# Hybrid decoder block on one core: FFN gate and up products with the weights as the loaded operand

## The reference

```python
def rmsnorm(x, g):
    y = xf * lax.rsqrt(jnp.mean(xf * xf, axis=-1, keepdims=True) + EPS)
    return (y * g)
def swiglu(h, wg, wu, wd):
    return (jax.nn.silu(h @ wg) * (h @ wu)) @ wd      # wg, wu 2048 x 5632, wd 5632 x 2048
...
        x = x + 0.5 * swiglu(rmsnorm(x, ffn1_norm[i]), ffn1_wg[i], ffn1_wu[i], ffn1_wd[i])
        x = x + hybrid_mixer(rmsnorm(x, mix_norm[i]), ...)
        x = x + 0.5 * swiglu(rmsnorm(x, ffn2_norm[i]), ffn2_wg[i], ffn2_wu[i], ffn2_wd[i])
    return rmsnorm(x, final_norm)
```

## Time and profile before

| | |
|---|---|
| median of 3 runs | 1923.17 us (1922.71 to 1926.27) |
| span of the profiled execution | 1920.8 us |
| TensorE busy | 1906.4 us, 99%, 8715 matmuls |
| TensorE loads | 1562.8 us, 81% |
| VectorE busy | 997.9 us, 52% |
| ScalarE busy | 899.3 us, 47% |
| first FFN | to about 739 us |
| mixer | about 739 to 1188 us |
| second FFN | from about 1188 us |
| memory | 350.96 MB, mean 183 GB/s |

### The profile page before, as it was taken

The page is one execution under the profiler, slowest core; times in us unless marked ns, Lnnn a source line. Parts: engine busy times, 40 slices in busy tenths (PEclk is TensorE's granted clock), DMA queues, the critical chain, the costliest instruction groups (busy, mean ns, idle before and its releaser), DMA issues.

```text
span 1920.8 us, 23438 instructions
## 1 busy us (share of the span) xinstructions
PE 1906.4 (99%) x8715; PEld 1562.8 (81%) x8715; DVE 997.9 (52%) x1070; ACT 899.3 (47%) x1127; POOL 15.5 (1%) x24
## 2 busy tenths in 40 slices
PE   9999999999999999999999999999999999999998
PEld 7888888888888888887778778888888888888886
DVE  5445544544544444556665776544544445445444
ACT  6444444544444444444454546445444444444443
POOL 1000000000000000000000000000000000000000
PEclk9999999999999999999999999999999999999999
DMA  7555665566555556554435645665565555566664
GB/s 257 192 189 183 188 197 183 179 199 191 190 183 197 196 189 193 172 171 129 114 95 169 187 158 166 199 195 175 187 202 191 192 189 176 196 219 195 192 192 144
DMA packets 185947, 350.96 MB, mean 183 GB/s; under 512 B 13140, under 2 KB 17984, under 8 KB 185760
## 3 DMA queue, kind: packets, MB, share of 16 engines
q1 hardware_dynamic: 183264, 349.22, 56.8%
q10 hardware_dynamic: 2240, 0.47, 0.1%
q0 software_dynamic: 384, 0.47, 0.1%
HBM read 348.01 MB, written 2.10 MB: 182 GB/s over the span
## 4 chain that ended last, share of the span: by engine, by line
PE 97%; DVE 2%; ACT 1%; issue 0%; ACTq 0%; DVEq 0%
PE ps L459 30%; PE ps L461 30%; PE ps L460 30%; PE ps L480 3%; PE ps L625 1%; PE ps L645 1%; DVE w_lo L1164 1%; PE ps L626 0%; ACT w_hi L841 0%; PE ps L519 0%; PE ps L718 0%; DVE p_h L1433 0%; ACT junk L868 0%; DVE x L1229 0%; ACT hT_hi L855 0%
## 5 line engine op out<-in xcount | busy, mean ns | idle before, releaser
L1164 DVE TENSOR_TENSOR w_lo<-raw,w_hi 128x1024 fp32r<-128x1024 f32 x656 | 789.7, 1223 | 662.0 <-ACT w_hi L841 659.7
L841 ACT ACTIVATE w_hi<-raw 128x1024 fp32r<-128x1024 f32 x656 | 682.0, 1060 | 593.3 <-PE ps L461 517.2
L459 PE MATMUL ps<-w_hi,hT_hi 128*128 128x512 f32 x1760 | 690.9, 393 | 1.2 <-DVE w_lo L1164 1.1
L461 PE MATMUL ps<-w_hi,hT_lo 128*128 128x512 f32 x1760 | 685.6, 390 | 0.0
L460 PE MATMUL ps<-w_lo,hT_hi 128*128 128x512 f32 x1760 | 685.3, 389 | 0.0
L459 PEld LDWEIGHTS ps<-w_hi,hT_hi 128*128 128x128 f32 x1760 | 330.8, 188 | 69.1 <-issue 1.4
L461 PEld LDWEIGHTS ps<-w_hi,hT_lo 128*128 128x128 f32 x1760 | 330.4, 188 | 69.1
L460 PEld LDWEIGHTS ps<-w_lo,hT_hi 128*128 128x128 f32 x1760 | 330.7, 188 | 66.5
L459 PE MATMUL ps<-w_hi,guT_hi 128*128 128x512 f32 x704 | 274.5, 390 | 0.0
L461 PE MATMUL ps<-w_hi,guT_lo 128*128 128x512 f32 x704 | 274.0, 389 | 0.0
L460 PE MATMUL ps<-w_lo,guT_hi 128*128 128x512 f32 x704 | 273.9, 389 | 0.0
(11 more groups left out here) (197 smaller groups left out, 799.7 us busy)
## 6 DMA issues: line engine op xcount, KB each, us to landing
raw<-in_ffn_wg_dram SPq DMA_DIRECT2D x176, 512.0 KB, 4.5
raw<-in_ffn_wu_dram SPq DMA_DIRECT2D x176, 512.0 KB, 4.5
raw<-in_ffn_wd_dram SPq DMA_DIRECT2D x176, 512.0 KB, 4.7
raw<-in_w_in_dram SPq DMA_DIRECT2D x88, 512.0 KB, 3.8
raw<-in_w_out_dram SPq DMA_DIRECT2D x32, 512.0 KB, 4.5
raw<-in_cmp_k_w_dram SPq DMA_DIRECT2D x8, 256.0 KB, 3.3
raw<-in_cmp_v_w_dram SPq DMA_DIRECT2D x8, 256.0 KB, 4.0
out_dram<-y_fin SPq DMA_DIRECT2D x8, 256.0 KB, 3.1
```

The lines of the kernel that those rows point to most:

```text
L459: mm(o, x_hi, w_hi[:, s, kk, :], start=first and kk == 0, stop=False)
L461: ins = mm(o, x_lo, w_hi[:, s, kk, :], start=False, stop=last and kk == GK - 1)
L841: act.activation(w_hi[:, c % SLOTS, :, :], raw[:, c % SLOTS, :, :], ACT.Copy).then_inc(hi_ready, 1)
L1164: tt(w_lo[:, s, :, :], raw[:, s, :, :], w_hi[:, s, :, :].bitcast(F32), ALU.subtract).then_inc(lo_ready, 1)
```

## The change

For gate and up, the operands change places: the loaded operand is a 128x128 tile of the weights (w_hi or w_lo), the moving operand the 256 tokens of hT. The result has hidden features on the partitions and tokens along the bank, four tiles of 128 features in two banks, just as the down product wants it. `gu_transposes` and its banks' use go away. A group of these jobs is now 24 loads and matmuls of 256 columns, where it was 12 of 512.

The token scale rs now lies along the free axis. After the first gate job of each FFN a row form of it is made: VectorE spreads rs to rs_rows, TensorE transposes the two pieces into bank 7, ScalarE copies bank 7 to rs_cols. VectorE multiplies the gate result with rs_cols into gu (`gate`), ScalarE takes silu of gu in SBUF in one instruction, VectorE multiplies with the up result (`up`), ScalarE copies to guT_hi and VectorE makes guT_lo, all as 128x1024. The up result's own factor rs and the 0.5 are applied in the residual (half_rs, per token), since they are common to all hidden features of a token.

```diff
+        rs_rows_ready = sem("rs_rows_ready")
...
+            def ff_job(c, pair, i=None, per=0, after={}, before={}):
+
+                for j in range(JD):
+                    for f in before.get(j, ()):
+                        f()
+                    pe.wait_ge(lo_ready, count(c + j + 1, i, per))
+                    s = (c + j) % SLOTS
+                    for kk in range(GK):
+                        k = GK * j + kk
+                        for n in range(CH // P):
+                            o = ps[:, 2 * pair + n // 2, n % 2 * TOK:n % 2 * TOK + TOK]
+                            f_hi = w_hi[:, s, kk, n * P:n * P + P]
+                            f_lo = w_lo[:, s, kk, n * P:n * P + P]
+                            mm(o, f_hi, hT_hi[:, k, :], start=k == 0 and n % 2 == 0, stop=False, skip_group_check=True)
+                            mm(o, f_lo, hT_hi[:, k, :], start=False, stop=False, skip_group_check=True)
+                            ins = mm(o, f_hi, hT_lo[:, k, :], start=False, stop=k == KD - 1, skip_group_check=True)
+                    ins.then_inc(group_done, 1)
+                    for f in after.get(j, ()):
+                        f()
...
-            def gu_transposes(f, n, i=None):
-                pe.wait_ge(gu_done, count(2 * (NFC * f + n + 1), i, 2))
-                for b in range(2):
-                    to_bank(4 + b, operand_use("gu", f, b, n), i, 1)
-                    transposes(4 + b, [(kk * TOK + t * P, gu[:, t, (2 * b + kk) * P:][:, 0:P])
-                                       for kk in range(2) for t in range(NT)])
...
+            def rs_columns(f):
+
+                pe.wait_ge(rs_rows_ready, f + 1)
+                if f == 1:
+                    to_bank(7, seen[7])
+                for t in range(NT):
+                    ins = pe.transpose(ps[:, 7, t * P:t * P + P], rs_rows[:, t, :], ident)
+                ins.then_inc(rs_cols_full, 1)
...
-                job(c, JD, hT_hi, hT_lo, 0, after=after, before=before)
+                ff_job(c, 0, after=after, before=before)
+                rs_columns(f)
                 c += JD
                 with pe.Fori(0, NFC - 1) as i:
-                    job(c, JD, hT_hi, hT_lo, 1, i, 2 * JD)
-
-                    pe.wait_ge(silu_done, count(2 * (NFC * f + 1), i, 2))
-                    job(c + JD, JD, hT_hi, hT_lo, 0, i, 2 * JD, after={3: [lambda: gu_transposes(f, 0, i)]})
+                    ff_job(c, 1, i, 2 * JD)
+
+                    pe.wait_ge(gate_read, count(NFC * f + 1, i, 1))
+                    ff_job(c + JD, 0, i, 2 * JD)
+
+                    pe.wait_ge(gu_done, count(NFC * f + 1, i, 1))
...
+            def rs_columns(f):
+
+                act.wait_ge(rs_cols_full, f + 1)
+                act.activation(rs_cols[:, :], ps[:, 7, 0:TOK], ACT.Copy).then_inc(rs_cols_ready, 1)
+
+            def silu(f, n, i=None):
+
+                act.wait_ge(gate_read, count(NFC * f + n + 1, i, 1))
+                act.activation(gu[:, :, :], gu[:, :, :], ACT.Silu).then_inc(silu_done, 1)
...
                 job(c, JD, after=after)
+                rs_columns(f)
                 c += JD
                 with act.Fori(0, NFC - 1) as i:
-                    job(c, JD, i, 2 * JD, after={1: [lambda: silu(f, 0, c, i)]})
-                    job(c + JD, JD, i, 2 * JD, after={5: [lambda: gu_operand(f, 0, i)]})
+                    job(c, JD, i, 2 * JD, after={2: [lambda: silu(f, 0, i)]})
+                    job(c + JD, JD, i, 2 * JD, after={3: [lambda: gu_operand(f, 0, i)]})
...
+            def ffn_scales(f):
+
+                phase = RS_FFN2 if f else RS_FFN1
+                nc.vector.tensor_scalar(half_rs[:, f, :], rs[:, phase, :], 0.5, None, ALU.mult)
+                for t in range(NT):
+                    ins = nc.vector.tensor_copy(rs_rows[:, t, :], rs[:, phase, t:t + 1].to_broadcast([P, P]))
+                ins.then_inc(rs_rows_ready, 1)
+
+            def gate(f, n, done, i=None):
+
+                dve.wait_ge(group_done, count(done, i, 2 * JD))
+                dve.wait_ge(rs_cols_ready, f + 1)
+                tt(gu[:, :, :], ps[:, 0:2, :].rearrange("p b (k t) -> p (b k) t", t=TOK),
+                   rs_cols[:, :].unsqueeze(1).to_broadcast([P, CH // P, TOK]), ALU.mult).then_inc(gate_read, 1)
...
                 job(c, JD, after=after)
+                ffn_scales(f)
                 c += JD
                 with dve.Fori(0, NFC - 1) as i:
-                    job(c, JD, i, 2 * JD)
+                    job(c, JD, i, 2 * JD, after={1: [lambda: gate(f, 0, c, i)]})
                     job(c + JD, JD, i, 2 * JD, after={1: [lambda: up(f, 0, c + JD, i)],
-                                                      5: [lambda: gu_operand(f, 0, i)]})
+                                                      3: [lambda: gu_operand(f, 0, i)]})
...
-            half = lambda t: 0.5
+            halves = [lambda t: half_rs[:, 0, t:t + 1], lambda t: half_rs[:, 1, t:t + 1]]
```

More of the change, by code:

```diff
@@ L176, in build_program @@
     rs = sb("rs", [P, 6, NT])
+    half_rs = sb("half_rs", [P, 2, NT])
+    rs_rows = sb("rs_rows", [P, NT, P])
+    rs_cols = sb("rs_cols", [P, TOK])
     junk = sb("junk", [P, CONV], BF16)
@@ L288, in build_program @@
         rs_done = sem("rs_done")
+        rs_rows_ready = sem("rs_rows_ready")
+        rs_cols_full = sem("rs_cols_full")
+        rs_cols_ready = sem("rs_cols_ready")
+        gate_read = sem("gate_read")
         silu_done = sem("silu_done")
         gu_done = sem("gu_done")
+        gu_hi = sem("gu_hi")
+        gu_lo = sem("gu_lo")
         resid_done = sem("resid_done")
@@ L551, in ffn @@
                     else:
-                        before = {}
+                        if n == 1:
+                            pe.wait_ge(gu_done, NFC * (f + 1))
                         if f == 0:
@@ L878, in root @@
                 act.activation(var[:, phase, :], var[:, phase, :], ACT.Sqrt).then_inc(root_done, 1)
[L880 to L896 removed]
+            def rs_columns(f):
[4 more added lines that the diff above has]
+                act.activation(gu[:, :, :], gu[:, :, :], ACT.Silu).then_inc(silu_done, 1)
+            def gu_operand(f, n, i=None):
+                act.wait_ge(gu_done, count(NFC * f + n + 1, i, 1))
+                k = 4 * n
+                dst = guT_hi[:, k:k + 4, :] if i is None else guT_hi[:, bass.ds(i * 4 + k, 4), :]
+                act.activation(dst, gu[:, :, :], ACT.Copy).then_inc(gu_hi, 1)
             def ffn(f):
@@ L925, in ffn @@
                     if n == 0:
[L926 removed]
+                        after = {3: [lambda: gu_operand(f, NFC - 1)]}
                         if f == 0:
@@ L1264, in ffn @@
                     if n == 0:
-                        after = {1: [lambda: up(f, NFC - 1, c)], 5: [lambda: gu_operand(f, NFC - 1)]}
+                        after = {1: [lambda: up(f, NFC - 1, c)], 3: [lambda: gu_operand(f, NFC - 1)]}
                     else:
-                        after = {1: [lambda: residual(n - 1, c + JF * n, (n - 1) % 2, half)]}
+                        after = {1: [lambda: residual(n - 1, c + JF * n, (n - 1) % 2, halves[f])]}
                         if f == 0:
@@ L1549, in put @@
                     after.setdefault(c, []).extend(fs)
-                put(MIX0 + 1, lambda: residual(NDC - 1, MIX0, 1, half))
+                put(MIX0 + 1, lambda: residual(NDC - 1, MIX0, 1, halves[0]))
                 put(MIX0 + 3, lambda: variance(RS_MIX, DM, 2 * NDC))
@@ L1625, in _ @@
                 xs = x[:, t, DM - CH:DM]
-                stt(out=xs, in0=ps[:, 2 + t, :], scalar=0.5, in1=xs, op0=ALU.mult,
+                stt(out=xs, in0=ps[:, 2 + t, :], scalar=half_rs[:, 1, t:t + 1], in1=xs, op0=ALU.mult,
                     op1=ALU.add).then_inc(resid_done, 1)
```

70 lines of the change are left out of this document (24 added, 46 removed).

## The result

| | before | after |
|---|---|---|
| median, lowest to highest | 1922.94 us, 1922.71 to 1926.27 | 1972.71 us, 1972.24 to 1972.88 |
| span of the profiled execution | 1920.8 us | 1970.4 us |
| matmuls on TensorE | 8715 | 12767 |
| one iteration of the FFN loop | 44.42 us | 46.08 us |

The changed kernel is slower: 1.0257 times the time before, 95% interval 1.0242 to 1.0271. The forecast was 1913.0 us with a range up to 1938. What came is the top of the bound that the prediction had put on its largest term, and two smaller losses.

What follows compares the result with a forecast made beforehand. TensorE's own work was taken to bound the kernel. From the profiled 1920.8 us, -19.6 for transposes, +9.3 for pauses, 0 for narrow pairs and +0.1 for the residual gave 1910.6, plus 2.4 made 1913.0 us; range 1906 to 1938, 80%.

Steps and rivals of the forecast that it cites:

- The bound: Whole kernel: TensorE, busy for 99% of the span, sets the time, so changes are priced as its work or standstill.
- Transposes removed: FFN loop: dropping the 176 transposes of gated activations gives back 0.89 us in each of 22 chunks, -19.6 us.
- Narrow pairs: FFN gate and up groups: 8448 pairs of 256 columns replace 4224 of 512, at 113.4 ns each, cost 0.
- rival A: FFN gate and up: narrow pairs take more than half a wide one, 1935 us at 116 ns, 1969 at 120; 26%.
- the nearest rows: Mixer gate product, 48 loaded columns at 113.3 ns, and one full load beside a 256-column stream, 0.11 to 0.12 us; decided for 0.
- The sign that the prediction had named for being wrong: FFN loop: an iteration above 44.0 us, or idle time inside it; 43.5 us was expected, not 44.42.
- the fixed part of about 2.5 ns for each matmul: 4224 additional FFN matmuls: 10.6 us by the skill's rule, giving 1923.6 us; set aside because the trace showed exactly half.
- The pause: After each FFN's first gate job: the scales' copy delays weight splits, so TensorE loses 4.65 us, +9.3 us for two FFNs.
- Rival C: Both FFN pauses: the clock falls, about 2 us lost at each, 1917 us; 7%.
- Rival B: FFN loop body outgrows TensorE's instruction store, a fetch at each of 18 backward branches, +36 to +72 us, 1949 to 1985; 7%.
- The covers: FFN loop: VectorE's gate scaling, silu from SBUF and later load issues finish before TensorE needs the weights, at no cost.
- The sum: Whole kernel: 1920.8 - 19.6 + 9.3 + 0.1 = 1910.6, and + 2.4 = 1913.0 us, 0.5% faster.

Runs made afterwards that it cites:

- the stretches: Kernel before, with runs of 48 load-and-matmul pairs of various sizes and formats appended behind its last product, results unused; 128 loaded, 256 moving columns took 120.1 ns a pair.
- the run with the filler: Changed kernel with 16 useless wide matmuls on TensorE in each pause behind the first gate job of an FFN: 1969.01 us.

## Why the prediction was wrong

**The bound** was right: TensorE's own work sets the time, before and after.

**Transposes removed, -19.6 us.** Right in kind and nearly in size: -18.7 by the run without them, and 22 x 0.90 = 19.8 by its loop.

**Narrow pairs, taken at 113.4 ns and 0 us.** This is the step that failed. The term is +54.7 us, measured by itself with the tokens still loaded, and 120 ns for each pair: the upper bound that the prediction had worked out (13.4 ns fixed, +56 us) was the value, and rival A at its top the case that came. The choice between the bounds went by "the nearest rows". The earlier trace rows were like the new pair in the moving side and the format, but loaded 48 columns, and the stretches show that with 256 moving columns 32 to 80 loaded ones are cheaper than a full load. The earlier trace rows had the full load, but in one instance at the page's resolution of 10 ns, where the question was 113 or 120; it was a narrow stream between a 48-column load and a wide stream, and one 0.11 beside one 0.12 can't tell them apart. Against these two stood 4224 pairs of the very load in question, at 226.7 ns, which is 13.4 ns above 512 columns at the full clock. The prediction computed that number and used it as a bound only. A repeated price of the operation itself should have outweighed a cheaper one of a different shape, or at least have left the two about equally likely; 55 to 26 was too sure, and the range ended at 116.3 ns. The sign that the prediction had named for being wrong, an iteration above 44.0 us, came: 46.08.

The prediction had also written down that the fixed part of about 2.5 ns for each matmul, from the Trainium skill, "TensorE: Matmul & The Clock Gate", section "Back-to-back issue gap", was not in the trace. The stretches show that it is there in bfloat16 (109.5 and 215.9 ns, 2.8 and 2.6 above the columns' time) and that this format has some 13 instead.

**The pause, 4.65 us at each of two places.** Right: from the two transposes at 35.84 to the first up matmul at 40.50 it is 4.66 us, with the steps in the order given (copy at 36.26, table load at 36.84, splits from 38.13 and 39.22). In the second FFN the same distance is 4.48. TensorE's idle time in them is 4.27 and 4.10 us.

**The clock.** Rival C came as well, beside A: the clock fell in both pauses. At the first place it stayed up for 4.0 us of the idle time, as the row at the end of the trace has it, and fell shortly before the pause was over; at the second it fell after 2.1 us, so that row is no rule. The price given to rival C, about 2 us for each place, was near: 1.5 and 2.2 by the rows, 3.7 by the run with the filler.

**The instruction store.** Rival B did not come: one packet in the 400 us of looping from 80 us on, in a body of about 790 instructions, and 46 on the page against 40.

**The covers** (VectorE's scaling of the gate, silu from SBUF, later load issues) held: from 80 to 480 us TensorE was busy for all 400.00 us.

**The sum.** 1922.9 + 54.7 - 18.7 + 12.9 = 1971.8 us, each term from a run of its own; measured 1972.7. With 120 ns in place of 113.4, and the fall of the clock, the prediction's own sum would have been 1913.0 + 56 + 4 = 1973.

## What to carry to other kernels

When an operation is split into more and smaller ones, divide what it takes now into streaming time (columns over the clock) and the rest, and count the rest once for each new one; let a cheaper row of another shape overrule this only if its loaded size and format are the same and it is read over many repeats. In a kernel whose matrix engine is busy throughout, halving the moving side to save transposes pays only if the fixed parts of all new pairs are below the transposes: here 54.7 us against 18.7. And a preparation put at the front of another engine's queue drains the work that this engine had ahead; the same step two places later cost nothing.

## What the runs showed of the hardware

- In the 4-byte reduced format a load-and-matmul pair with 128 loaded columns takes its columns over 2.4 GHz and 13 to 16 ns, from 256 to 512 moving columns (120.1 ns at 256, 203.0 at 448, 227.4 at 512).
- Below 256 moving columns it gets cheaper only down to 112 ns: 192 and 240 moving columns both took that, about the 111 to 112 ns from one full load to the next.
- At the low clock, 128 and 256 moving columns take the same: 213 ns in the stretch, 213 to 214 behind the pause.
- A load of fewer columns is not cheaper with 512 moving ones: 230 to 232 ns for 32, 64 or 96, against 227 for 128.
- A single bfloat16 pair between 4-byte ones costs 26 ns more than the pairs at their own prices, where the shorter format gives 10.9. Putting the passes of one format together took 11.3 and 16.2 us off.
- In two pauses of TensorE of 4.27 and 4.10 us the granted clock fell to 0.5, after some 4.0 and 2.1 us of idle time, for 3.4 and 6.8 us; with useless matmuls in the pause it did not fall. It fell once without any idle time as well, 4.5 us into a stretch of pairs with 64 moving columns.
